# Columns of a modulation matrix loaded from ScalarE's queue instead of SyncE's, in a three-layer mixer kernel

## The chip, the cores and the metric

The kernel runs on one core of a Trainium2 chip. The metric is the device time of the whole program in microseconds, the median of several executions. The profiled execution is one more, taken by the hardware profiler; all times of rows below are its own, counted from its start.

## What is computed

A token stream x of 512 tokens by 2048 channels goes through three layers, all in 32-bit floats. Each layer takes a modulation from a condition vector, a product with a wide weight matrix, a mixer, a product back and a residual. In short:

```python
mod = silu(c) @ w_ada + b_ada                 # 2048 -> 3 x 2048: shift, scale, gate
h = norm(x) * (1 + scale) + shift
z = h @ w_in                                  # layer 1: 7184 columns
y = concat(spatial_gating(z...), forgetting_attention(z...)) @ w_out
x = x + gate * y
# layer 2: gated linear attention, both directions, with states from a context of
# 256 tokens (the context has a modulation of its own from a vector c_ctx), and a
# convolution of three taps; layer 3: means over windows of rows, four 512 x 512 products
x = layer_norm(alpha * x + gate * mixer(x * (1 + scale) + shift))
```

The modulation is a matrix-vector product: w_ada has 2048 rows and 6144 columns in each of the three layers, so it is as large as other weights, and each of its elements is used once (twice where the context needs the same columns).

## The kernel before, in words

All large products are written as a list of *groups* (GROUPS). A group is 512 output columns (or fewer) of one weight matrix, summed over 16 *tiles* of 128 rows. Each 32-bit weight tile is split into a high and a low part, and each product is three matmuls (high by high, high by low, low by high, L1010 to L1012 or L1019 to L1021). With four column blocks a tile is 12 matmuls; in the group f (112 columns) and in r (128 columns) it is 3, in ck (256 tokens) 6.

A tile goes through the engines so. SyncE loads pairs of tiles into w_raw, four pairs deep (`weights`, L292). ScalarE copies a tile to its high part in w_hi (L547, L571), four tiles ahead of TensorE. VectorE subtracts to make the low part in w_lo (L1399), after the high part. TensorE waits for the low part (`lo_done`) and for the operand's tile (`op_tile`). The high part of tile k is made when TensorE is done with tile k-4, so ScalarE's and VectorE's *step t* of a group works on tile t+4, for the last four steps on the next group's tiles.

The modulation's columns are computed beside these products. 28 groups have a *part*: 512 columns of w_ada, in 16 tiles. They are five runs of consecutive groups: va to the first v group (8 groups), gb to the third wo1 group (5), the first ck group alone (1), r to the first ev group (6), and the second egb group to the third xp group (8). In step t of such a group VectorE, after the low part, adds tile t of the part, scaled by the condition's entry, to an accumulator (`part_tile`, L1402, instructions L1415 for tile 0 and L1417 else; two per tile where the context's condition is added too). The columns come in pairs of tiles into a_raw, two pairs deep, so pair m may be loaded when tile 2m-3 has been accumulated, and it is wanted at tile 2m. After the group TensorE sums the accumulator over partitions, and VectorE takes the result (`take_part`).

Before the change SyncE issues these loads too (`modulation`, L303). Its `stream` issues the weight pairs of a group in order and puts the modulation pair m-3 behind weight pair m (LAG is 3), the last three pairs behind the next group's first weight pairs. SyncE waits on `part_tile` for the buffer before it issues. For `beside` (the groups of the gated attention's heads) a_raw holds other data, which SyncE writes to memory.

Where a group is the first to use an operand (va, wo1, r, wo2, xp), the operand's tiles are built while its steps run: ScalarE makes op_hi (L594), VectorE op_lo (L1498), and steps start at operand tile 4 (`early`). ScalarE also evicts most groups' results from PSUM at their end (L686 for va).

Of the kernel before, what the change touches and what calls it, by code (L numbers as in the profile page):

```python
# [5 lines left out]
P = 128  # L6
# [3 lines left out]
KT = D // P  # L10
GC = 512
# [6 lines left out]
GLA_HEADS, DK = 4, 256  # L18
# [3 lines left out]
RAW = 4  # L22
# [58 lines left out]
GROUPS, FIRST, CHUNKS = plan()  # L81
# [28 lines left out]
def early(n):  # L110


    if n and GROUPS[n - 1]["operand"] == GROUPS[n]["operand"] or GROUPS[n]["name"] == "cr":

        return 0
    return min(GROUPS[n]["kt"], KT - 4)
# [30 lines left out]
class Build:  # L147
# [42 lines left out]
    def at(self, word, *shape):  # L190
        n = 1
        for k in shape:
            n *= k
        assert word + n <= ARENA, (word, shape)
        v = self.arena[:, word:word + n]
        if len(shape) == 2:
            v = v.rearrange("p (a b) -> p a b", a=shape[0])
        if len(shape) == 3:
            v = v.rearrange("p (a b c) -> p a b c", a=shape[0], b=shape[1])
        return v  # L200

    def sem(self, name):
        if name not in self.sems:
            self.sems[name] = self.nc.alloc_semaphore(name)
        return self.sems[name]
# [9 lines left out]
def ordinal(n):  # L215

    return sum(x["part"] is not None for x in GROUPS[:n])
# [14 lines left out]
def sync_program(B, sp):  # L232
    A, sem, at = B.A, B.sem, B.at
# [35 lines left out]
    w_ada = A["w_ada"][0].rearrange("(k p) n -> p k n", p=P)  # L269
# [22 lines left out]
    def weights(n, m, r=0):  # L292

        g = GROUPS[n]
        slot = (g["kc"] // 2 + m) % RAW
        if g["kc"] + 2 * m >= 2 * RAW:

            sp.wait_ge(sem("lo_done"), r * 8 + (g["kc"] + 2 * m - 2 * RAW + 2))
        tiles = slice(2 * m, 2 * m + 2) if isinstance(r, int) else bass.ds(r * 8 + 2 * m, 2)
        sp.dma_start(B.w_raw[:, slot, :, 0:g["width"]],  # L300
                     B.weight(g)[:, tiles, g["col"]:g["col"] + g["width"]]).then_inc(B.w_in[slot], 16)

    def modulation(n, m):  # L303

        part, o = GROUPS[n]["part"], ordinal(n)
        if part is None:
            return
        src = A["w_ada"][0] if part < 12 else A["w_ada_2"][(part - 12) // 12]
        src = src.rearrange("(k p) n -> p k n", p=P)
        c = part % 12 * GC  # L310
        if o or m >= 2:

            sp.wait_ge(sem("part_tile"), KT * o + 2 * m - 2)
        sp.dma_start(B.a_raw[:, m % 2, :, :], src[:, 2 * m:2 * m + 2, c:c + GC]).then_inc(B.a_in[m % 2], 16)

    def stream(n, middle=None):


        pairs = GROUPS[n]["kt"] // 2
        before = n and GROUPS[n - 1]["part"] is not None  # L320
        if GROUPS[n]["part"] is None and not before and not middle and pairs == 8 and GROUPS[n]["name"] != "egb":
            with sp.Fori(0, 2) as r:
                for m in range(4):
                    weights(n, m, r)
            return
        for m in range(pairs):
            weights(n, m)
            if GROUPS[n]["name"] == "egb":
                conv_loads(GROUPS[n]["i"], m)
            if m < LAG and before and not (middle and m == 2):  # L330
                modulation(n - 1, 8 - LAG + m)
            if middle and m == 1:

                if before:
                    modulation(n - 1, 7)
                middle()
            if m >= LAG:
                modulation(n, m - LAG)

    def residual(n):  # L340

# [82 lines left out]
    def conv_loads(i, m):  # L424

        if i == 0 and m == 3:

            sp.wait_ge(sem("heads_done"), GLA_HEADS + 1)
            beside_store(1, GLA_HEADS - 1)
            sp.wait_ge(sem("beside_stored"), 16 * (2 * GLA_HEADS + 1))  # L430
        j = m - 3 if i == 0 else m + 5
        if 0 <= j < 8:
            if j >= CONV_SLOTS:

                sp.wait_ge(sem("conv_done"), j - CONV_SLOTS + 1)
            src = B.c_sp.rearrange("p (v h) (t s) -> p v (h t) s", v=4, t=4)
            sp.dma_start(at(AT_CONV, CONV_SLOTS, 4, S)[:, j % CONV_SLOTS, :, :], src[:, :, j, :])\
                .then_inc(B.sem(f"conv_in_{j}"), 16)
# [8 lines left out]
    for n, name in enumerate(names):  # L447
# [7 lines left out]
        if name in ("ua", "ga"):  # L455
            if g["i"] == 0:
                with sp.Fori(0, 2) as r:
                    attention_turn(r, name == "ga")
            continue
        stream(n, middles.get(n))  # L460
        if name == "xp" and g["i"] == 0:
            spill_stream(2)
# [36 lines left out]


N_ROW_LOADS = 12
LAG = 3


def start_step(n):
# [27 lines left out]
def scalar_program(B, act):  # L533
    nc, sem, at, ps, Y = B.nc, B.sem, B.at, B.ps, B.Y
# [4 lines left out]
    def high_tile(c, width):  # L539
        raw, fill = c // 2 % RAW, c // (2 * RAW)  # L540
        if c % 2 == 0:

            act.wait_ge(B.w_in[raw], 16 * (fill + 1))
        if c >= RING:

            act.wait_ge(sem("w_used"), c - RING + 1)
        Act(B.w_hi[:, c % RING, 0:width], B.w_raw[:, raw, c % 2, 0:width], ACT.Copy).then_inc(sem("hi_done"), 1)  # L547

    def step(n, t):

        c, k, width = GROUPS[n]["kc"], GROUPS[n]["kt"], GROUPS[n]["width"]
        after = GROUPS[n + 1]["width"] if n + 1 < len(GROUPS) else 0
        if t < k - 4:
            high_tile(c + 4 + t, width)
        elif after:
            high_tile(c + 4 + t, after)

    def ahead(n):

        c, k, width = GROUPS[n]["kc"], GROUPS[n]["kt"], GROUPS[n]["width"]  # L560
        after = GROUPS[n + 1]["width"] if n + 1 < len(GROUPS) else 0
        if k == KT and after == width and not early(n):
            with act.Fori(0, 2) as r:
                for t in range(c + 4, c + 12):
                    raw = t // 2 % RAW
                    if t % 2 == 0:

                        act.wait_ge(B.w_in[raw], r * 16 + 16 * (t // (2 * RAW) + 1))

                    act.wait_ge(sem("w_used"), r * 8 + (t - RING + 1))  # L570
                    Act(B.w_hi[:, t % RING, 0:width], B.w_raw[:, raw, t % 2, 0:width],  # L571
                        ACT.Copy).then_inc(sem("hi_done"), 1)
        else:
            for t in range(early(n), k):
                step(n, t)

    def conv_ahead(n):

        for t in range(KT):
            high_tile(GROUPS[n]["kc"] + 4 + t, GC)  # L580
            for j in range(8):
                if CONV_AT[j] == (GROUPS[n]["i"], t):
                    act.wait_ge(sem(f"conv_in_{j}"), 16)
                    x = at(AT_CONV, CONV_SLOTS, 4, S)[:, j % CONV_SLOTS, 3, :]
                    Act(x, x, ACT.Silu).then_inc(sem("conv_gate"), 1)

    def split_hi(operand, src, tok=S, tiles=KT, ready=None):

        if operand:

            last = max(x["kc"] + x["kt"] for x in GROUPS if x["operand"] == operand - 1)
            act.wait_ge(sem("w_used"), last)
        for t in range(tiles):
            Act(B.op_hi[:, t, 0:tok], src(t), ACT.Copy).then_inc(sem("op_high"), 1)  # L594
            if 4 <= t < 4 + early(first_use(operand)):
                step(first_use(operand), t - 4)
# [68 lines left out]
    for n, g in enumerate(GROUPS):  # L665
        name, i = g["name"], g["i"]
# [8 lines left out]
        if name == "egb":  # L675
            conv_ahead(n)
        else:
            ahead(n)
# [78 lines left out]
    for t in range(NT):  # L757
        for j in range(4):
            k = 4 * t + j
# [1276 lines left out]
def model_kernel(nc, A, out):  # L2036
    B = Build(nc, A, out)
    with nc.Block() as block:

        @block.sync  # L2040
        def _(sp):
            with nc.allow_non_contiguous_dma(reason="columns of small tables"):
                sync_program(B, sp)

        @block.gpsimd
        def _(pool):
            pool_program(B, pool)

        @block.scalar
        def _(act):  # L2050
            scalar_program(B, act)

        @block.vector
        def _(dve):
            vector_program(B, dve)

        @block.tensor
        def _(pe):
            tensor_program(B, pe)
# [38 lines left out]
```

## Time and profile before

| | |
|---|---|
| median of 3 runs | 3188.45 us (3185.68 to 3190.76) |
| the profiled execution's own time | 3190.58 us |
| its span in the profile | 3188.8 us |
| TensorE busy with matmuls | 2874.2 us, 90% |
| VectorE busy | 1772.7 us, 56% |
| ScalarE busy | 1054.5 us, 33% |
| moved by DMA | 451.17 MB, mean 141 GB/s |

The span is the profile's, the execution's own time is 1.8 us longer. Instructions that only issue a DMA or wait are not counted as busy. Groups start about every 44 us where a tile is 12 matmuls.

### The profile page before, as it was taken

Reading aid. Unit: us, or ns where it says so; the run is one execution under the profiler, and the core shown is the slowest. Engines: PE = TensorE matmul, PEld = TensorE weight load, DVE = VectorE, ACT = ScalarE, POOL = GpSimd, SP = SyncE. Lnnn points to the kernel's source line nnn. Section 1 sums busy time; section 2 is a strip of 40 time slices with the busy share of each in tenths; the row PEclk is TensorE's granted clock in tenths of the full one; section 3 lists DMA queues with packets and bytes.
Section 4 is the critical chain, followed back from the end, with each engine's and each line's share of the span. In section 5 each row is a group of like instructions: output and inputs, shape, how many; then the busy total and the mean of one; then the engine's idle time right before and its main releaser. Section 6 shows DMA issues by size and latency. Waiting matters only on the chain.

```text
span 3188.8 us, 36906 instructions
## 1 busy us (share of the span) xinstructions
PE 2874.2 (90%) x12667; PEld 2275.4 (71%) x12667; DVE 1772.7 (56%) x2777; ACT 1054.5 (33%) x1630; POOL 4.1 (0%) x10
## 2 busy tenths in 40 slices
PE   3499999989999988689999999999899699998995
PEld 2377887666777857468878686776788488887883
DVE  7857773444578536264427475473766576324443
ACT  2333222333323235332224434352332332223224
POOL 0000000000000000000000000000000000000000
PEclk8699999999999989789999999999999899999997
DMA  9766552212255526165532222223656274332331
GB/s 369 280 195 206 192 173 70 62 61 66 85 185 191 193 94 198 69 222 191 192 113 80 73 92 66 86 92 106 225 191 210 80 246 144 99 95 91 113 113 53
DMA packets 219351, 451.17 MB, mean 141 GB/s; under 512 B 23753, under 2 KB 29339, under 8 KB 214861
## 3 DMA queue, kind: packets, MB, share of 16 engines
q1 hardware_dynamic: 219212, 449.36, 42.6%
q8 instruction: 83, 1.36, 0.2%
q14 instruction: 56, 0.45, 0.0%
HBM read 422.01 MB, written 27.30 MB: 141 GB/s over the span
## 4 chain that ended last, share of the span: by engine, by line
PE 81%; DVE 6%; ACT 4%; issue 4%; DVEq 1%; DMA 1%; ACTq 1%; SPq 1%; PEldq 0%; PEld 0%
PE ps L1010 20%; PE ps L1012 19%; PE ps L1011 19%; PE ps L1019 4%; PE ps L1020 4%; PE ps L1021 4%; PE ps L1341 2%; PE ps L1063 2%; PE ps L1211 1%; PE ps L1219 1%; PE ps L989 1%; DVE acc L1584 1%; PE ps L1372 1%; PE ps L1375 1%; PE ps L1363 1%
## 5 line engine op out<-in xcount | busy, mean ns | idle before, releaser
L1010 PE MATMUL ps<-op_hi,w_hi 128*128 128x512 f32 (+2 forms) x2928 | 1177.1, 402 | 84.2 <-DVE op_lo L1498 43.7
L1012 PE MATMUL ps<-op_hi,w_lo 128*128 128x512 f32 (+2 forms) x2928 | 1154.5, 394 | 0.0
L1011 PE MATMUL ps<-op_lo,w_hi 128*128 128x512 f32 (+2 forms) x2928 | 1154.4, 394 | 0.0
L1399 DVE TENSOR_TENSOR w_lo<-w_raw,w_hi 128x512 fp32r<-128x512 f32 (+2 forms) x640 | 421.7, 661 | 620.9 <-ACT w_hi L571 414.3
L1010 PEld LDWEIGHTS ps<-op_hi,w_hi 128*128 128x128 f32 (+1 forms) x2928 | 560.7, 192 | 225.2 <-issue 54.4
L1012 PEld LDWEIGHTS ps<-op_hi,w_lo 128*128 128x128 f32 (+1 forms) x2928 | 559.6, 191 | 119.8
L1011 PEld LDWEIGHTS ps<-op_lo,w_hi 128*128 128x128 f32 (+1 forms) x2928 | 561.0, 192 | 112.7 <-issue 1.7
L571 ACT ACTIVATE w_hi<-w_raw 128x512 fp32r<-128x512 f32 x496 | 312.8, 632 | 969.4 <-PE ps L1012 802.6
L1417 DVE SCALAR_TENSOR_TENSOR acc<-a_raw,vec,acc 128x512 f32<-128x512 f32 x540 | 392.8, 746 | 19.6 <-DMA a_raw<-in_w_ada 19.5
L547 ACT ACTIVATE w_hi<-w_raw 128x512 fp32r<-128x512 f32 (+2 forms) x240 | 134.7, 565 | 357.6 <-PE ps L1012 276.2
L1019 PE MATMUL ps<-w_hi,op_hi 128*128 128x512 f32 x512 | 202.9, 396 | 27.4 <-DVE op_lo L1498 16.0
L1020 PE MATMUL ps<-w_hi,op_lo 128*128 128x512 f32 x512 | 201.3, 393 | 0.0
L1021 PE MATMUL ps<-w_lo,op_hi 128*128 128x512 f32 x512 | 201.0, 393 | 0.0
L1452 DVE TENSOR_TENSOR w_lo<-w_raw,w_hi 128x512 fp32r<-128x512 f32 x96 | 66.2, 693 | 161.0 <-ACT w_hi L571 160.7
L1019 PEld LDWEIGHTS ps<-w_hi,op_hi 128*128 128x128 f32 x512 | 97.3, 190 | 48.7 <-issue 16.2
L1879 DVE TENSOR_TENSOR w_lo<-w_raw,w_hi 128x512 fp32r<-128x512 f32 x128 | 83.3, 687 | 65.7 <-ACT w_hi L903 61.6
L1021 PEld LDWEIGHTS ps<-w_lo,op_hi 128*128 128x128 f32 x512 | 97.4, 190 | 20.7
L1020 PEld LDWEIGHTS ps<-w_hi,op_lo 128*128 128x128 f32 x512 | 97.4, 190 | 20.4 <-issue 0.2
L818 ACT ACTIVATE arena<-arena,small 128x128 f32<-128x128 f32 (+1 forms) x64 | 36.0, 563 | 195.0 <-DVE small L1811 195.0
L1584 DVE SCALAR_TENSOR_TENSOR acc<-arena,vec,acc 128x512 f32<-128x512 f32 x128 | 84.9, 743 | 22.6 <-ACT vec L658 11.5
L903 ACT ACTIVATE w_hi<-w_raw 128x512 fp32r<-128x512 f32 x128 | 75.7, 621 | 43.0 <-PE ps L1012 42.9
L938 ACT ACTIVATE arena<-arena 128x2048 f32<-128x2048 f32 x28 | 53.6, 1915 | 108.6 <-DVE arena L1925 108.6
(208 smaller groups left out, 2139.0 us busy)
## 6 DMA issues: line engine op xcount, KB each, us to landing
a_raw<-in_w_ada SPq DMA_DIRECT2D x224, 512.0 KB, 4.0
w_raw<-in_w_in_e SPq DMA_DIRECT2D x160, 512.0 KB, 4.6
w_raw<-in_w_in SPq DMA_DIRECT2D x112, 512.0 KB, 4.8
arena<-in_w_ada SPq DMA_DIRECT2D x64, 512.0 KB, 8.0
w_raw<-in_w_in_o SPq DMA_DIRECT2D x64, 512.0 KB, 3.7
w_raw<-in_w_out SPq DMA_DIRECT2D x32, 512.0 KB, 5.0
w_raw<-in_w_out_e SPq DMA_DIRECT2D x32, 512.0 KB, 4.9
w_raw<-in_w_out_o SPq DMA_DIRECT2D x32, 512.0 KB, 3.7
```

Of the source, the lines that this page charges most:

```text
L547: Act(B.w_hi[:, c % RING, 0:width], B.w_raw[:, raw, c % 2, 0:width], ACT.Copy).then_inc(sem("hi_done"), 1)
L571: Act(B.w_hi[:, t % RING, 0:width], B.w_raw[:, raw, t % 2, 0:width], ACT.Copy).then_inc(sem("hi_done"), 1)
L1010: mm(dst, hi[:, cols], B.op_hi[:, k, 0:tok], start=first, stop=False)
L1011: mm(dst, hi[:, cols], B.op_lo[:, k, 0:tok], start=False, stop=False)
L1012: last = mm(dst, lo[:, cols], B.op_hi[:, k, 0:tok], start=False, stop=last_t)
L1019: mm(dst, B.op_hi[:, k, rows], hi, start=first, stop=False)
L1020: mm(dst, B.op_lo[:, k, rows], hi, start=False, stop=False)
L1021: last = mm(dst, B.op_hi[:, k, rows], lo, start=False, stop=last_t)
L1399: V.tensor_tensor(B.w_lo[:, c % RING, 0:width], B.w_raw[:, c // 2 % RAW, c % 2, 0:width], B.w_hi[:, c % RING, 0:width].bitcast(f32), ALU.s ...
L1417: last = V.scalar_tensor_tensor(out=sums, in0=x, scalar=col, in1=sums, op0=ALU.mult, op1=ALU.add)
L1584: V.scalar_tensor_tensor(out=sums, in0=ring[:, s, v * GC:(v + 1) * GC], scalar=B.vec[:, bass.ds(r * 8 + (VEC["c"] + s), 1)], in1=sums, op0 ...
L1879: V.tensor_tensor(B.w_lo[:, c % RING, :], B.w_raw[:, c // 2 % RAW, c % 2, :], B.w_hi[:, c % RING, :].bitcast(mybir.dt.float32), ALU.subtract)\
```

## The change

The modulation loads are issued by ScalarE. In step t of a group with a part, behind the step's high part, it issues pair t/2 + 1 of that part for even t up to 12, and at t = 14 pair 0 of the next group's part if it has one. The first pair of a run's first group is issued at its step 0, just ahead of pair 1. ScalarE waits on `part_tile` as SyncE did. In the second egb group pairs 0 and 1 also wait until the last of a_raw's other data has been written to memory. SyncE issues weights alone; its groups with a part now run in a loop, ScalarE's groups with a part are written out.

```diff
@@ sync_program
-    def modulation(n, m):
-        ...
-        if o or m >= 2:
-            sp.wait_ge(sem("part_tile"), KT * o + 2 * m - 2)
-        sp.dma_start(B.a_raw[:, m % 2, :, :], src[:, 2 * m:2 * m + 2, c:c + GC]).then_inc(B.a_in[m % 2], 16)
 
     def stream(n, middle=None):
         pairs = GROUPS[n]["kt"] // 2
-        before = n and GROUPS[n - 1]["part"] is not None
-        if GROUPS[n]["part"] is None and not before and not middle and pairs == 8 and GROUPS[n]["name"] != "egb":
+        if not middle and pairs == 8 and GROUPS[n]["name"] not in ("egb", "wo2") and GROUPS[n]["kc"] >= 2 * RAW:
             with sp.Fori(0, 2) as r:
                 for m in range(4):
                     weights(n, m, r)
@@ 
             if GROUPS[n]["name"] == "egb":
                 conv_loads(GROUPS[n]["i"], m)
-            if m < LAG and before and not (middle and m == 2):
-                modulation(n - 1, 8 - LAG + m)
             if middle and m == 1:
-                if before:
-                    modulation(n - 1, 7)
                 middle()
-            if m >= LAG:
-                modulation(n, m - LAG)
@@ scalar_program
+    def modulation(n, m):
+        part, o = GROUPS[n]["part"], ordinal(n)
+        src = B.A["w_ada"][0] if part < 12 else B.A["w_ada_2"][(part - 12) // 12]
+        src = src.rearrange("(k p) n -> p k n", p=P)
+        c = part % 12 * GC
+        if GROUPS[n]["name"] == "egb" and m < 2:
+            act.wait_ge(sem("beside_stored"), 16 * (2 * GLA_HEADS + 1))
+        if o or m >= 2:
+            act.wait_ge(sem("part_tile"), KT * o + 2 * m - 2)
+        act.dma_start(B.a_raw[:, m % 2, :, :], src[:, 2 * m:2 * m + 2, c:c + GC]).then_inc(B.a_in[m % 2], 16)
+
+    def has_part(n):
+        return 0 <= n < len(GROUPS) and GROUPS[n]["part"] is not None
+
+    def modulation_step(n, t):
+        if t == 0 and has_part(n) and not has_part(n - 1):
+            modulation(n, 0)
+        if has_part(n) and t % 2 == 0 and t < 14:
+            modulation(n, t // 2 + 1)
+        if has_part(n) and t == 14 and has_part(n + 1):
+            modulation(n + 1, 0)
@@ step, ahead, conv_ahead
             high_tile(c + 4 + t, after)
+        modulation_step(n, t)
...
-        if k == KT and after == width and not early(n):
+        if k == KT and after == width and not early(n) and not has_part(n):
             with act.Fori(0, 2) as r:
```

## Rows read from the trace of the kernel before

**Rows 1.** The page, parts 1 and 4: busy time by engine, chain by engine.
```profile
PE 2874.2 (90%) x12667; PEld 2275.4 (71%) x12667; DVE 1772.7 (56%) x2777; ACT 1054.5 (33%) x1630; POOL 4.1 (0%) x10
...
PE 81%; DVE 6%; ACT 4%; issue 4%; DVEq 1%; DMA 1%; ACTq 1%; SPq 1%; PEldq 0%; PEld 0%
```

**Rows 2.** TensorE's waits: line, released by, us in total, times, longest.
```profile
PE ps L1010 <- DVE w_lo L1399: 13.7, 18, 3.1
```

**Rows 3.** Waits of SyncE's queue.
```profile
SPq L314 <- DVE acc L1417: 1052.2, 213, 54.4
```

**Rows 4.** The tile a_raw: instruction times in ns, idle time, DMA landing.
```profile
L314 SPq DMA_DIRECT2D a_raw<-in_w_ada x224: 367/368/1296, 115.7 to 2666.4; - x112
...
  DMA a_raw<-in_w_ada: 21.2, 20
...
DMA to landing us min/median/max: 3.7/4.0/12.3
```

**Rows 5.** Timeline of va: start, us, engine, line, instruction [idle before, released by].
```profile
138.20 0.61 ACT L547 ACTIVATE w_hi<-w_raw 128x512 fp32r<-128x512 f32 x1
...
139.54 0.48 DVE L1415 TENSOR_SCALAR acc<-a_raw,vec 128x512 f32<-128x512 f32 x1
...
142.84 0.63 ACT L547 ACTIVATE w_hi<-w_raw 128x512 fp32r<-128x512 f32 x1 [1.62 <-PE ps L1021]
...
145.52 0.69 DVE L1399 TENSOR_TENSOR w_lo<-w_raw,w_hi 128x512 fp32r<-128x512 f32 x1
...
150.94 0.63 ACT L547 ACTIVATE w_hi<-w_raw 128x512 fp32r<-128x512 f32 x1 [0.79 <-PE ps L1021]
```

**Rows 6.** Timeline of f and of the start of q.
```profile
223.91 0.37 SPq L314 DMA_DIRECT2D a_raw<-in_w_ada  x1
...
224.58 1.08 ACT L547 ACTIVATE w_hi<-w_raw 128x112 fp32r<-128x112 f32 x4
...
229.32 0.37 SPq L314 DMA_DIRECT2D a_raw<-in_w_ada  x1
...
233.22 0.75 DVE L1417 SCALAR_TENSOR_TENSOR acc<-a_raw,vec,acc 128x512 f32<-128x512 f32 x1 [0.91 <-DMA a_raw<-in_w_ada]
...
255.30 0.50 PE L1010 MATMUL ps<-op_hi,w_hi 128*128 128x512 f32 x1 [3.06 <-DVE w_lo L1399]
```

**Rows 7.** Timeline of the first ck group.
```profile
1204.61 2.17 ACT L571 ACTIVATE w_hi<-w_raw 128x512 fp32r<-128x512 f32 x4
...
1205.86 0.48 DVE L1415 TENSOR_SCALAR acc<-a_raw,vec 128x512 f32<-128x512 f32 x1
...
1211.78 0.75 DVE L1417 SCALAR_TENSOR_TENSOR acc<-a_raw,vec,acc 128x512 f32<-128x512 f32 x1 [1.04 <-DMA a_raw<-in_w_ada]
...
1228.03 0.75 DVE L1417 SCALAR_TENSOR_TENSOR acc<-a_raw,vec,acc 128x512 f32<-128x512 f32 x1 [0.21 <-DMA a_raw<-in_w_ada]
1228.70 0.69 DVE L1399 TENSOR_TENSOR w_lo<-w_raw,w_hi 128x512 fp32r<-128x512 f32 x1
```

**Rows 8.** Windows in ck: busy by engine, granted clock, DMA share, GB/s.
```profile
1215.00:1220.00 5.00, 5.00 (x24) 4.14 (x23) 4.21 (x7) 2.14 (x4) 0.00 (x0) 1.00 0.85 258
1220.00:1225.00 5.00, 5.00 (x24) 4.14 (x23) 3.64 (x6) 2.53 (x4) 0.00 (x0) 1.00 1.01 370
```

**Rows 9.** Timeline of r and of the start of ek.
```profile
1368.89 0.31 ACT L547 ACTIVATE w_hi<-w_raw 128x128 fp32r<-128x128 f32 x1 [4.64 <-DMA w_raw<-in_w_in_e]
...
1370.69 0.49 DVE L1415 TENSOR_SCALAR acc<-a_raw,vec 128x512 f32<-128x512 f32 x1 [1.18 <-DMA a_raw<-in_w_ada]
...
1392.13 0.47 PE L1010 MATMUL ps<-op_hi,w_hi 128*128 128x512 f32 x1 [0.35 <-issue]
```

**Rows 10.** Timeline of the second egb group and of the start of wo2.
```profile
2282.44 0.75 DVE L1417 SCALAR_TENSOR_TENSOR acc<-a_raw,vec,acc 128x512 f32<-128x512 f32 x1
...
2284.37 0.69 DVE L1399 TENSOR_TENSOR w_lo<-w_raw,w_hi 128x512 fp32r<-128x512 f32 x1
...
2312.39 0.76 PE L1010 MATMUL ps<-op_hi,w_hi 128*128 128x512 f32 x1 [9.30 <-DVE op_lo L1498]
```

More of the change, by code:

```diff
@@ L301, in weights @@
                      B.weight(g)[:, tiles, g["col"]:g["col"] + g["width"]]).then_inc(B.w_in[slot], 16)
-    def modulation(n, m):
[L305 to L310, printed above, removed]
-        if o or m >= 2:
-            sp.wait_ge(sem("part_tile"), KT * o + 2 * m - 2)
-        sp.dma_start(B.a_raw[:, m % 2, :, :], src[:, 2 * m:2 * m + 2, c:c + GC]).then_inc(B.a_in[m % 2], 16)
     def stream(n, middle=None):
         pairs = GROUPS[n]["kt"] // 2
-        before = n and GROUPS[n - 1]["part"] is not None
-        if GROUPS[n]["part"] is None and not before and not middle and pairs == 8 and GROUPS[n]["name"] != "egb":
+        if not middle and pairs == 8 and GROUPS[n]["name"] not in ("egb", "wo2") and GROUPS[n]["kc"] >= 2 * RAW:
             with sp.Fori(0, 2) as r:
@@ L501 @@
 N_ROW_LOADS = 12
-LAG = 3
 def start_step(n):
@@ L585, in conv_ahead @@
                     Act(x, x, ACT.Silu).then_inc(sem("conv_gate"), 1)
+            modulation_step(n, t)
     def split_hi(operand, src, tok=S, tiles=KT, ready=None):
```

## The prediction

> **What bounds the kernel now.** I read the page first. TensorE is busy for 90% of the span and makes 81% of the chain that ended last [rows 1]. So a change of load queues is worth only what it does where TensorE waits. The list of TensorE's waits comes next: the low parts of weight tiles (w_lo, VectorE, L1399) cost it 13.7 us in 18 waits on one line [rows 2]. They are few, and the timeline puts them where a modulation column is accumulated beside short tiles. The queue's own waits show the largest number, 1052.2 us in 213 waits of SyncE's L314 for VectorE's accumulation [rows 3]. The reader must not take it for a loss: a queue that waits costs nothing unless what stands behind it comes late. The tile view of a_raw has the size of the lateness: VectorE sat 21.2 us in 20 waits for these loads, a load takes 367 ns to issue and lands after 3.7 to 12.3 us, 4.0 in the median [rows 4].
>
> **Where there is cover.** VectorE makes low parts up to four tiles ahead of TensorE. In a group with 12 matmuls a tile a load that is late by three microseconds eats into that lead and nothing else. In groups with 3 or 6 matmuls a tile (f, ck, r) VectorE itself sets the pace, and lateness goes through.
>
> **What the change removes.** SyncE no longer waits for accumulation steps between weight loads. Weight slots become free at the low part of the same step, so each weight load goes out about one accumulation (0.7 us) plus one issue (0.4 us) earlier. Nothing in TensorE's 12-matmul groups waits for weights, so this is worth nothing there.
>
> **What it adds to ScalarE.** 224 issues of 0.37 us [rows 4] are 83 us. ScalarE is busy 33% [rows 1], mostly waiting for TensorE between tiles, so its idle time hides them. If an issue took the longest seen, 1.30 us [rows 4], an even step would still be 0.63 + 1.30 us, under the 2.7 us that 12 matmuls take (three tiles between 142.84 and 150.94 [rows 5]). ScalarE's new wait is for the accumulation of step t-1, which VectorE runs before the low part of step t. Behind it stand the high part of step t+1 and, at a group's end, the eviction. When VectorE catches up it needs about 1.26 us for a low part and an accumulation; ScalarE needs 0.37 + 0.63 us after the wait, so it stays ahead.
>
> **What it moves: the first loads of a run.** Before, a run's first two columns were loaded by SyncE while the former group still ran. Now they are issued at step 0 behind a high part, just before VectorE wants them. As price of one I take 3.9 us, from the issue at 229.32 to the accumulation that waited for it at 233.22 [rows 6]. There are five such starts.
> - va: high part at 138.20, accumulation at 139.54 [rows 5]. Issued 138.3 to 138.8, it lands at 142.2 to 142.7, so VectorE is 2.7 to 3.2 us late. The low part of tile 6 ends at 146.2, and TensorE asks for it at 150.94, when ScalarE's high part shows it done with tile 5 [rows 5]. The lead of 4.7 us covers this: 0, with 1.5 us to spare.
> - gb has 12 matmuls a tile and no operand to build, so more cover than va: 0.
> - ck (6 matmuls): high part 1204.61, accumulation 1205.86 [rows 7]. It lands at 1208.6 to 1209.1, +2.7 to +3.3 us. From there to the last low part at 1228.70 before took 22.84 us, of which 4.0 us were five waits for a_raw, the first 1.04 and the last 0.21 [rows 7]; 18.8 us is work. A load is issued two and a half tiles before its use, 3.15 us of work, so with a landing L each two loads cost L - 3.15 in waits; six loads cost 3(L - 3.15): 2.3 us at 3.9, 5.5 us at 5.0. The end is 1208.85 + 18.8 + 2.3 to 5.5 = 1229.9 to 1233.2, which is +1.2 to +4.5 less what VectorE had to spare (some 0.1 to 0.7). The DMA engines are full there (share 0.85 to 1.01) [rows 8], and two more loads fall into the stretch, but it also starts 2.9 us sooner. I take +2.1 (0.5 to 3.8).
> - r (3 matmuls, VectorE builds the operand): ScalarE's high part at 1368.89 itself waits 4.64 us for its weights. Issued at 1369.0 to 1369.2, the column lands at 1372.9 to 1373.1; before, 1370.69 [rows 9]. TensorE follows VectorE tile by tile until 1392.13 [rows 9]. I take +2.3 (2.0 to 3.5; the lower is the shortest landing of 3.7, the upper a landing of 5).
> - egb's second group: VectorE is late by an earlier evacuation, the load lands before it is wanted: 0.
>
> **The second load of each later group** is issued at step 0, behind the former group's eviction. Only f suffers: its column 1 went out at 223.91, now after the high part at 224.58, which stands behind the eviction of va's second group [rows 6]: +0.7 to +1.0. In f each pair of steps waits for its column (0.91 us at 233.22 [rows 6], one of eight), two buffers alternate, and the last pair uses the late one; VectorE's next work ends in TensorE's 3.06 us wait at 255.30 [rows 6]. So it goes through. A landing longer by 0.5 us would add 0.25 x 7 pairs; one of 3.7 us takes 0.7 away. I take +1.2 (0 to 2.8).
>
> **ScalarE held back.** In the second egb group VectorE has no idle time and its end sets TensorE's restart at 2312.39 after 9.30 us [rows 10]. ScalarE now waits for the accumulation that ends at 2283.2 (started 2282.44), issues, and has the high part ready at 2284.2; VectorE wants it at 2284.37 [rows 10]. It just fits; there are two such places. +0.2 (0 to 1.2, with 1.0 us issues).
>
> **Sum:** 0 + 0 + 2.1 + 2.3 + 1.2 + 0.2 = +5.8 us. The profiled execution took 3190.58 us (span 3188.8 and 1.8 around it), so its like after the change would be 3196.4; it stood 2.1 us over the median. Against the median of 3188.45 the forecast is 3194.2 us.
>
> **Two queues.** The landing of a_raw is the number in dispute. In the before trace the column goes out first and the weights 0.41 us behind it on one queue (229.32 and its like), now the weights go first by about a microsecond on another. The trace has no such pair, so the landing is bounded by the shortest of 3.7 us below, and above by 5 us, an estimate between the median of 4.0 and the longest of 12.3 [rows 4]. The Trainium skill (DMA: Bandwidth & Descriptors, Queues, rings and completion order) says that each DMA engine goes round-robin between queues by packets; by it the column would share the engines with the weights ahead of it, and the sum would lean to the contention case. The same page (Issuing engines are not separate DMA queues) says that issuing from several engines saves only issue time; by it alone the steady state would not change, and no run here shows either yet.
>
> **The rivals.**
> - Contention (18%): columns land after 5 us beside weights. Then ck +3.8, r +3.5, f +1.0 + 7 x 0.55 = +4.8, egb +1: +13, 3201.5 us. For it: a DMA share of 1.01 in ck [rows 8]. Against: the bytes are the same. It decides from a landing of 4.6 us on.
> - Cover holds (22%): the issue overlaps the high part, loads land in 3.7 us, ck's end is caught up; r alone and something of f stay: +2, 3190.5 us.
> - Faster (10%): a column no longer queues among weights. If it landed at once, f would lose its eight waits of about 0.9 us, -7.3 us, 3181 us with the starts hidden. It decides only if the landing falls from 3.9 to under 2.5 us, and the shortest of 224 was 3.7 [rows 4].
> - My forecast has 50%, with a range of its own of 3190.5 to 3198.
>
> **The numbers.** No change that can be told is within 0.2%, 3182.1 to 3194.8. The forecast lies at its upper edge: 27 of its 50 fall inside, 23 above. Same 0.27 + 0.22 = 0.49; slower 0.23 + 0.18 = 0.41; faster 0.10. The range 3186 to 3203 leaves out most of the faster case and the tail of contention.
>
> **What would show it.** Right: VectorE's first accumulation in ck near 1209 and in r near 1373, counted from the same high parts, each with a wait for a_raw of some 3 us; no new TensorE stall in va, gb, wo1, wo2, xp; TensorE's restart after f one microsecond later. Wrong: a TensorE stall inside a 12-matmul group, ScalarE's high parts held for more than 1 us where VectorE then waits, issues on ScalarE far over 0.5 us, or a landing that leaves 3.7 to 4.6 us.

## The result, and the profile after

The changed kernel took 3202.74 us (median of 5 runs, 3200.66 to 3204.54) against 3188.45 us: a ratio of 1.0044, with a 95% interval of 1.0029 to 1.0059. It is slower by 14.3 us (9 to 19). The forecast was 3194.2 us with a range of 3186 to 3203, so the time lies 0.3 us inside the range's upper end. Slower had a chance of 0.41, the same time had 0.49. The profiled execution has a span of 3201.2 us, 12.4 us more than before.

I read the page first: busy time by engine, then the chain by engine.

```profile
PE 2879.8 (90%) x12667; PEld 2278.4 (71%) x12667; DVE 1772.8 (55%) x2777; ACT 1053.5 (33%) x1630; POOL 4.1 (0%) x10
...
PE 79%; DVE 6%; ACT 4%; issue 4%; DMA 3%; DVEq 1%; ACTq 1%; SPq 1%; PEldq 0%; PEld 0%
```

The work is the same as before [rows 1]; DMA went from 1% to 3% of the chain. The tile view of a_raw says which DMA. Its columns are those of [rows 4], and below them stands who waited.

```profile
L539 ACTq DMA_DIRECT2D a_raw<-in_w_ada x224: 374/374/483, 137.0 to 2678.6; - x112
...
  DMA a_raw<-in_w_ada: 41.5, 29
...
  ACT w_hi L525: 44.6, 16
...
  ACT op_hi L600: 15.4, 5
...
DMA to landing us min/median/max: 3.7/4.6/16.5
```

An issue takes 374 ns on ScalarE, 7 ns more than on SyncE. A load lands after 4.6 us in the median instead of 4.0, and after 16.5 us at worst. VectorE waited 41.5 us for these loads instead of 21.2. TensorE's waits for low parts:

```profile
PE ps L1016 <- DVE w_lo L1405: 20.8, 18, 3.9
```

That is 7.1 us more than [rows 2], in as many waits. To place the loss I took pairs of events that both timelines have and subtracted the lengths between them. The names used below are: *f*, from TensorE's first matmul of va at 132.06 us (times of the kernel before) to its first of q at 255.30; *ck*, from 1206.00 to the context's first product at 1293.28; *context*, from there to 1341.18; *r*, from 1362.21 to 1662.09; *xp*, from 2539.89, TensorE's first matmul of xp, to 2897.60. They are 1.41, 1.03, 1.70, 2.20 and 5.74 us longer. Outside these names two stretches of the changed kernel's profile differ by more than 0.5 us, both along with another granted clock of TensorE: from 1662.09 to 2539.89 it is 1.83 us shorter, from 2897.60 to 2948.84 it is 0.74 us longer (last section). The largest is one that the prediction priced at nothing. Here is the first xp group in the changed kernel's timeline:

```profile
2563.14 0.39 ACTq L539 DMA_DIRECT2D a_raw<-in_w_ada  x1
2563.21 0.34 SPq L290 DMA_DIRECT2D x_spill<-Y  x1
...
2579.67 0.75 DVE L1423 SCALAR_TENSOR_TENSOR acc<-a_raw,vec,acc 128x512 f32<-128x512 f32 x1 [10.25 <-DMA a_raw<-in_w_ada]
...
2583.19 0.63 ACT L600 ACTIVATE op_hi<-arena 128x512 fp32r<-128x512 f32 x1 [9.66 <-DVE acc L1423]
```

SyncE issues a 4 MB store of x (`spill_stream(2)`, the line behind the first xp group's `stream`) 0.07 us after ScalarE issued a column pair. The pair lands 16.5 us later, when the store is through. VectorE, which builds the operand in the same steps, stands for 10.25 us, and so does ScalarE behind its wait for the accumulation. TensorE waits 3.90 us for a low part, which is the longest of the row above. That is not yet 5.74 us; the rest is in TensorE's clock. Behind the wait it drops to the lower of its two levels. These are 3.4 us of the changed kernel, and the same 3.4 us of the kernel before, 5.70 us earlier (columns as in [rows 8]):

```profile
2583.00:2586.40 3.40, 3.40 (x10) 2.63 (x9) 3.40 (x7) 2.19 (x4) 0.00 (x0) 0.51 0.86 284
```

```profile
2577.30:2580.70 3.40, 3.40 (x17) 2.81 (x16) 1.65 (x3) 0.63 (x1) 0.00 (x0) 1.00 1.05 397
```

TensorE gets through 10 matmuls instead of 17. Half speed for 3.4 us costs 1.7 us, and 3.90 + 1.7 is 5.6. All six profiles in which TensorE stands still for 3.8 to 4.3 us here have this drop behind it (changed, e2, e7, e9, e10, e12), none of the other eight has it.

This is the same place in the kernel before:

```profile
2557.42 0.37 SPq L314 DMA_DIRECT2D a_raw<-in_w_ada  x1
...
2562.07 0.37 SPq L314 DMA_DIRECT2D a_raw<-in_w_ada  x1
...
2562.48 0.47 SPq L290 DMA_DIRECT2D x_spill<-Y  x1
...
2579.05 0.75 DVE L1417 SCALAR_TENSOR_TENSOR acc<-a_raw,vec,acc 128x512 f32<-128x512 f32 x1 [4.99 <-DMA a_raw<-in_w_ada]
```

The changed kernel is 5.72 us late when it comes to this place. The column at 2557.42 goes out at 2563.14 there, exactly as much later (TensorE's first matmul of xp, at 2539.89, is 5.73 us later): ScalarE is not late with it. The store at 2562.48 would fall on 2568.20 and stands at 2563.21, 5.0 us early. Before, SyncE's wait for accumulation step 5, ahead of column pair 4, had held the store back; the change took the wait away with the load.

How the two transfers share the engines stands in the DMA view of a window, here 2569 to 2571 us, in the middle of the store (queue 1 is SyncE's, queue 10 ScalarE's; the columns are packets, MB, and the time they took as a share of 16 engines' time):

```profile
q1 hardware_dynamic: 30, 0.98, 114.9%
q10 hardware_dynamic: 30, 0.06, 8.4%
```

The queues get the same number of packets, 30 and 30; in the windows of 2 us beside it they are 19 and 19, 19 and 20, 29 and 28. A packet of the store is 0.98 MB / 30 = 33 KB, a whole row of x (16 tiles of 2 KB). A packet of the column is 2 KB. So the column gets a sixteenth of the bytes. The store has 128 such packets and the column 256: taking turns one for one, the column is not through before the store is. The Trainium skill (DMA: Bandwidth & Descriptors, Queues, rings and completion order) has the rule, round-robin between queues by packets, and the trace agrees packet by packet; by that rule the price hangs on the length of a row.

### The profile page after: what moved, and what is told of

It reads as the page before. It is cut to its first block, busy times and chain, and to the rows that moved or that the text cites. A ratio compares the mean times of both kernels' runs of the same rounds, so it can differ in the third digit from the quotient of the medians.

```text
span 3201.2 us, 37322 instructions
## 1 busy us (share of the span) xinstructions
PE 2879.8 (90%) x12667; PEld 2278.4 (71%) x12667; DVE 1772.8 (55%) x2777; ACT 1053.5 (33%) x1630; POOL 4.1 (0%) x10
## 4 chain that ended last, share of the span: by engine, by line
PE 79%; DVE 6%; ACT 4%; issue 4%; DMA 3%; DVEq 1%; ACTq 1%; SPq 1%; PEldq 0%; PEld 0%
PE ps L1016 19%; PE ps L1018 19%; PE ps L1017 19%; PE ps L1025 3%; PE ps L1027 3%; PE ps L1026 3%; DMA a_raw<-in_w_ada 2%; PE ps L1347 2%; PE ps L1069 2%; PE ps L1217 1%; PE ps L1225 1%; PE ps L995 1%; PE ps L1378 1%; PE ps L1381 1%; DVE acc L1590 1%
## 5 line engine op out<-in xcount | busy, mean ns | idle before, releaser
L525 ACT ACTIVATE w_hi<-w_raw 128x512 fp32r<-128x512 f32 (+2 forms) x560 | 335.3, 603 | 1001.3 <-PE ps L1018 813.5
L576 ACT ACTIVATE w_hi<-w_raw 128x512 fp32r<-128x512 f32 x176 | 111.2, 632 | 317.9 <-PE ps L1018 228.2
L909 ACT ACTIVATE w_hi<-w_raw 128x512 fp32r<-128x512 f32 x128 | 75.7, 622 | 44.3 <-PE ps L1018 44.3
```

## The experiments

The theories: A, SyncE's removed waits let the store (and the weights) go ahead of the columns. B, ScalarE's own waits and issues in front of its high parts cost the time. C, two queues in themselves make a landing longer. P, a column's share beside a store follows from the length of the packets; Q, a store blocks a load whatever its packets.

Each ratio is to the kernel before in the same set, with its 95% interval. The changed kernel has 1.0044 and, run again (last but two), 1.0043, some 14 us; an interval is about 3 us wide on either side. So the stretches of the profiles decide between theories, and the ratios the sums. The table has the five named stretches, in us longer than in the kernel before's profile. They hold steps of the clock too: the stretches between them move by up to 4.8 us from profile to profile (255.30 to 1206.00 in e5, shorter), in kernels of both kinds, so a difference of less than 2 us in one profile is not a finding by itself.

| run | ratio | f | ck | context | r | xp |
|---|---|---|---|---|---|---|
| changed | 1.0044 | 1.41 | 1.03 | 1.70 | 2.20 | 5.74 |
| e10, changed again | 1.0043 | 2.93 | 0.90 | 1.70 | 2.25 | 5.73 |
| e1, store waits | 1.0017 | 1.88 | 1.26 | 1.70 | 2.30 | 1.17 |
| e2, starts early | 1.0027 | 2.75 | 0.91 | 1.70 | -1.29 | 5.81 |
| e3, SyncE's waits kept | 1.0029 | 3.20 | 2.73 | 0.01 | 3.10 | 1.13 |
| e4, before, store first | 1.0006 | 0.66 | -0.12 | 1.70 | -0.02 | 0.63 |
| e5, store in rows of 2 KB | 1.0019 | 3.61 | 1.27 | 3.40 | 2.29 | -0.09 |
| e12, store in 8 pieces | 1.0033 | 2.34 | 1.48 | 1.70 | 2.36 | 5.83 |
| e6, starts and later store | 1.0004 | 3.67 | 1.47 | 1.70 | -1.47 | 0.79 |
| e7, f and ck by SyncE | 1.0023 | 1.04 | 1.24 | 1.69 | 1.93 | 6.19 |
| e9, two issues a pair | 1.0039 | 2.61 | 1.40 | 1.70 | 2.10 | 5.82 |
| e11, three mends | 1.0001 | 0.16 | 1.18 | 1.70 | -1.45 | -0.21 |
| e8, before, r early | 0.9984 | 0.63 | -0.23 | 3.40 | -1.59 | -0.04 |

**e1: the store waits again.**

```diff
         if name == "xp" and g["i"] == 0:
+            sp.wait_ge(sem("part_tile"), KT * ordinal(n) + 6)
             spill_stream(2)
```

> The changed kernel with one wait more: SyncE issues the 4 MB store of x in the first xp group only when VectorE has accumulated tile 5 of that group's part, where it stood before the change. Theory A (the store overtook the columns, because SyncE no longer waited for accumulations): VectorE's wait of 10.25 us for a_raw and TensorE's of 3.90 us in the operand's build go, 5 to 6 us less than the changed kernel, about 3197 us; a shorter wait of some 5 us may come back at tile 8 or 10. Theory B (ScalarE, with its waits and issues in front of its own high parts, is what costs the time there): nothing changes, 3202 to 3203 us.

Ratio 1.0017 (1.0008 to 1.0026), 3196.59 us: some 8 us less than the changed kernel, of which xp has 4.6. Theory A holds. The timeline shows what is left of it:

```profile
2567.07 0.34 SPq L290 DMA_DIRECT2D x_spill<-Y  x1
2567.07 0.42 ACTq L540 DMA_DIRECT2D a_raw<-in_w_ada  x1
...
2581.48 0.75 DVE L1424 SCALAR_TENSOR_TENSOR acc<-a_raw,vec,acc 128x512 f32<-128x512 f32 x1 [7.88 <-DMA a_raw<-in_w_ada]
```

The next pair is caught in its place, for 14.4 us, but it is wanted two steps later, when most of the operand is built, and TensorE loses 1.2 us instead of 5.7.

**e4: in the kernel before, the store ahead of a column.**

```diff
             weights(n, m)
+            if GROUPS[n]["name"] == "xp" and GROUPS[n]["i"] == 0 and m == 7:
+                spill_stream(2)
...
-        if name == "xp" and g["i"] == 0:
-            spill_stream(2)
```

> The kernel before, with one thing changed: in the first xp group SyncE issues the store of x right behind weight pair 7, ahead of column pair 4 instead of behind it. If the store's place alone is what costs, column pair 4 lands only with the store, 12 us or more after its issue, VectorE waits some 5 to 6 us at tile 8 of the operand's build and the kernel is 1 to 5 us slower than before, 3190 to 3194 us. If it takes the second queue, nothing is lost: 3188.5 us.

Ratio 1.0006 (0.9997 to 1.0015): xp is 0.63 us longer. Column pair 4, issued at 2562.02 behind the store on the same queue, is used at 2575.88 after a wait of 7.31 us. So one queue delays a column as a second one does (13.8 us); what costs little here is that pair 3 was already out at 2557.37. The loss needs both, the early store and a column that is not clearly ahead of it: here pair 3 was 0.93 us ahead on the store's own queue and landed after 4.4 us, in the changed kernel it was 0.07 us ahead on another queue and landed after 16.5 us.

**e3: SyncE keeps its waits, without the loads.**

```diff
+    def modulation(n, m):
+        part, o = GROUPS[n]["part"], ordinal(n)
+        if part is not None and (o or m >= 2):
+            sp.wait_ge(sem("part_tile"), KT * o + 2 * m - 2)
```

> The changed kernel, but SyncE keeps all its waits for accumulation steps where they stood before the change, without the loads. Theory A (weights and the store go out too early, ahead of the columns): the store's 5.7 us go, and what f (1.4 us) and ck (1.0 us) lost goes too, since a weight pair again follows a column instead of leading it: 8 us less, about 3194.5 us, the rest being the late start of r. Theory C (two queues in themselves make a landing longer): the median landing of a_raw stays 4.6 us, only the store's part goes, 3197 us. Theory B (ScalarE's holding): 3202 us or more, since a wait is added.

Ratio 1.0029 (1.0018 to 1.0040). xp came back, as A and C had it. But f and ck did not, they became longer (3.20 and 2.73), and the median landing rose to 5.1 us. With its waits SyncE issues the weights in the same moment in which ScalarE issues the column. Two loads of 512 KB then share the engines, and the column is the one that lands last: taking away the weights' lead brings neither f nor ck back. The traces show what that does to a column and the weight pair issued next to it, in medians:

| | column lands after | weights land after | both are there, from the first issue |
|---|---|---|---|
| before: one queue, column 0.4 us ahead (200 pairs) | 4.0 us | 4.9 us | 5.3 us |
| changed: two queues, weights 0.3 to 0.7 us ahead (52 pairs) | 4.7 us | 3.9 us | 5.2 us |
| e3: two queues, within 0.15 us of each other (107 pairs) | 5.3 us | 4.7 us | 5.3 us |

So theory C holds in part only. The column lands later, but the two loads together take as long on two queues as on one. What the second queue changes is who comes home first: on one queue the column did, because SyncE issued it first; now the weights do, and over the whole program their median landing fell from 4.7 to 3.7 us while the column's rose from 4.0 to 4.6. No stretch is shorter for it. Whether a column issued 0.4 us ahead on ScalarE's queue would land after 4.0 us again was not run.

**e2: the runs at ck and r start a group early.**

```diff
+        if GROUPS[n]["name"] == "cr" or GROUPS[n]["name"] == "cv" and GROUPS[n]["i"] == 1:
+            if t in (10, 12):
+                modulation(n + 1, t // 2 - 5)
+            return
```

> The changed kernel, with pairs 0 and 1 of the runs that start at ck and r issued by ScalarE at steps 10 and 12 of the group before. If late starts cost what the prediction says, r's first accumulation waits no longer than before the change (3.38 us to 1.2 or none) and TensorE starts ek 2.0 to 3.5 us sooner; in ck the trace of the changed kernel shows no wait at the first accumulation, so nothing there. Together 2 to 3.5 us less than the changed kernel, 3199 to 3201 us. The rival, that r is held by its weights, which stand behind the stores of x and of the states: the high part at 1374 waits as long and only 0 to 1 us is won.

Ratio 1.0027 (1.0017 to 1.0037), 5 us less than the changed kernel. r is 3.5 us shorter, ck as long as it was. In the changed kernel r's start looks like this:

```profile
1373.98 0.31 ACT L525 ACTIVATE w_hi<-w_raw 128x128 fp32r<-128x128 f32 x1 [4.38 <-DMA w_raw<-in_w_in_e]
1373.98 0.90 ACTq L539 DMA_DIRECT2D a_raw<-in_w_ada  x2
...
1377.99 0.49 DVE L1421 TENSOR_SCALAR acc<-a_raw,vec 128x512 f32<-128x512 f32 x1 [3.38 <-DMA a_raw<-in_w_ada]
```

and with the pair issued early, beside a high part that still waits 4.38 us for its weights:

```profile
1373.24 0.48 DVE L1426 TENSOR_SCALAR acc<-a_raw,vec 128x512 f32<-128x512 f32 x1
```

VectorE no longer waits. The kernel before had lost 1.3 us there as well: its column stood behind r's weights and these behind the stores of x and of the states.

**e5: the store in rows of 2 KB.**

```diff
+        if m == 2:
+            for t in range(KT):
+                sp.dma_start(B.x_sp[:, t, :], B.Y[:, t, :]).then_inc(sem("spilled"), 16)
+            return
```

> The changed kernel; the store of x in the first xp group stands where the change put it, but goes out as 16 stores of one tile each, so that a row of it is 2 KB, as long as a row of a column pair, and not 32 KB. Theory P (two queues share the DMA engines packet by packet, so a column of short packets gets a small share beside a store of long ones: 522 packets with 1.02 MB against 679 with 5.23 MB in the window of the store): the column issued with the store lands after 5 to 8 us instead of 16.5, VectorE waits 0 to 2 us instead of 10.25, TensorE not at all, 5 us less than the changed kernel. Theory Q (a store blocks a load whatever its packets): the wait of 10 us stays, and the time with it.

Ratio 1.0019 (1.0010 to 1.0028); xp is as short as before (-0.09).

```profile
2561.88 0.39 ACTq L543 DMA_DIRECT2D a_raw<-in_w_ada  x1
...
2569.32 0.75 DVE L1427 SCALAR_TENSOR_TENSOR acc<-a_raw,vec,acc 128x512 f32<-128x512 f32 x1 [1.16 <-DMA a_raw<-in_w_ada]
```

The column lands after 7.4 us, in a window in which the engines are nearly as full (DMA share 0.88 from its issue to its landing, 0.96 in the changed kernel's like window). Theory P has its number. This run changed the length of a row and the size of a piece together, so the next one changes the piece alone.

**e12: the store in 8 pieces of 16 partitions, rows as long as they were.**

```diff
+            for d in range(8):
+                rows = slice(16 * d, 16 * d + 16)
+                sp.dma_start(B.x_sp[rows, :, :], B.Y[rows, :, :]).then_inc(sem("spilled"), 16)
```

> The changed kernel; the store of x in the first xp group goes out as 8 stores of 16 partitions each (512 KB, the size of a column pair), whose rows stay 32 KB long. The run with rows of 2 KB changed two things at once, the length of the rows and the size of a piece; this one changes the piece alone. If the length of the rows decides how the engines are shared (theory P), the column issued with the store lands after 12 to 17 us as in the changed kernel and the xp stretch stays 4 to 6 us longer than before. If it is the piece, it lands after 5 to 9 us and the stretch is within 1 us of before.

Ratio 1.0033 (1.0020 to 1.0046). Neither answer came clean. The column lands after 8.0 us (issued at 2560.38, used at 2568.34), against my 12 to 17. Yet xp stays 5.83 us longer. The window from 2566 to 2568 us shows why the column got through:

```profile
q1 hardware_dynamic: 31, 0.49, 147.3%
q10 hardware_dynamic: 208, 0.39, 50.9%
```

ScalarE's queue gets 208 packets here, and the store's has 15 of 32 KB (the 0.49 MB; the other 16 of its 31 are under 512 bytes). So the turns one for one hold only while both queues have packets waiting. A piece has 16 rows, as many as there are engines, and between pieces ScalarE's queue has them to itself. The row of 32 KB still goes in one packet, but few others stand behind it. By these two runs the column's price is the length of a row times the rows that are queued; that is a reading, no run varied the number of queued rows alone. The store became the slow one: its issues stretch over 21.4 us and its last piece lands 29.9 us after the first issue, instead of 15.9 us, the second group's weights stand behind it, ScalarE waits 10.82 us for them before it can make a high part, and TensorE stands still for 3.99 us, with the clock's drop behind it:

```profile
2591.68 0.63 ACT L530 ACTIVATE w_hi<-w_raw 128x512 fp32r<-128x512 f32 x1 [10.82 <-DMA w_raw<-in_w_in_o]
...
2593.13 0.47 PE L1021 MATMUL ps<-op_hi,w_hi 128*128 128x512 f32 x1 [3.99 <-issue]
```

So this stretch is as long as the changed kernel's for another reason.

**e7: the columns beside f and ck issued by SyncE.** `modulation`, with its waits, is back in SyncE's `stream` at its old places and returns at once for other groups; ScalarE's returns for these.

```diff
+        if GROUPS[n]["name"] not in ("f", "ck") or GROUPS[n]["part"] is None:
+            return
```

> The changed kernel, but the columns beside the two short-tile groups f and ck are issued by SyncE with its waits, as before the change; all others stay with ScalarE. If two queues that share the engines are what makes a landing longer beside 512 KB weights, f and ck give back what they lost, 1.4 and 1.0 us in the profile: 2.4 us less than the changed kernel, and no landing over 4.3 us in these groups. If the loss there came of ScalarE's held-back high parts, the same. If it was the scatter of one profile, f and ck stay where they are.

Ratio 1.0023 (1.0014 to 1.0033). f is 1.04 us longer than before, and ck 1.24. Over all profiles, f has 0 to 1.04 where SyncE issues (before, e4, e7, e8, e11; mean 0.50) and 1.41 to 3.67 where ScalarE does (nine profiles, mean 2.71). They do not overlap: f costs 2.2 us. VectorE's own waits for a_raw in f say the same without the clock in them: 5.5 to 6.2 us in the five profiles with SyncE, 7.7 to 9.5 us in the nine with ScalarE, 7.67 against 5.48 in the changed kernel. For ck the answer is open: 0.90 to 1.48 with ScalarE (nine profiles without e3, mean 1.21), -0.23 to 0 in three profiles with SyncE, but 1.24 in this one, where VectorE waits 2.01 us for one column. VectorE's waits for a_raw in ck add up to 2.9 to 5.0 us in the four profiles with SyncE and to 5.2 to 5.8 us in the nine with ScalarE. I had expected no landing over 4.3 us in these groups; in ck they go up to 6.5 us on SyncE's queue too. The time is some 7 us less than the changed kernel's by the ratios, of which the profile's f and ck show 0.2 us; the rest is not explained.

**e9: two issues for each pair.**

```diff
+        for h in range(2):
+            act.dma_start(B.a_raw[:, m % 2, h, :], src[:, 2 * m + h, c:c + GC]).then_inc(B.a_in[m % 2], 16)
```

> The changed kernel, with each column pair loaded by two issues of one tile instead of one of two tiles: 448 issues on ScalarE instead of 224, some 83 us more of its queue's time, the same bytes. If the issues are hidden in ScalarE's idle time, as the prediction has it, the time stays within 3 us of the changed kernel. If ScalarE's queue is a cost in itself (0.4 us a pair in front of high parts that are wanted), the operand builds and the short-tile groups lengthen by 0.4 us a pair, 20 to 30 pairs, 8 to 12 us in all.

Ratio 1.0039 (1.0025 to 1.0052), the changed kernel's within its interval. An issue took 453 ns in the median, so ScalarE spent over 100 us more. Against the changed kernel's two profiles the only stretch that is clearly longer is ck, by 0.4 us, and the 8 to 12 us that a costly issue would have added are not there. ScalarE's time is free here, to some 3 us.

**e10: the changed kernel again.**

> The changed kernel once more, with nothing changed, beside the others of this set: a ratio to the kernel before of 1.003 to 1.005. In the second profile the stretches show what is scatter: xp +5.7 us and r +2.2 us against the kernel before should come again, f between +1.4 and +3.7 us, ck between +0.9 and +2.7 us; the context stretch between 1293 and 1341 us is scatter if it moves by a microsecond or more.

Ratio 1.0043 (1.0029 to 1.0056). xp, r and the context stretch repeat to 0.05 us, f does not (1.41 and 2.93). Of f's difference 0.57 us lies in the first 8 us of va, with which the stretch begins (granted clock 0.79 and 0.73), and 1.05 us in VectorE's waits for a_raw in f (7.67 and 8.72 us).

**e6, e11: the mends together.** e6 is e2 with the store behind weight pair 2 of the second xp group. e11 is e2 and e5, with f's columns issued by SyncE.

```diff
+        if GROUPS[n]["name"] == "xp" and GROUPS[n]["i"] == 1:
+            for m in range(8):
+                weights(n, m)
+                if m == 2:
+                    spill_stream(2)
+            return
```

> The changed kernel with both mends: ck's and r's first two column pairs are issued one group early by ScalarE, and the store of x goes behind weight pair 2 of the second xp group, some 10 us later. The first has won 3.5 us against the changed kernel in the stretch from r's first matmul to 1662 us, the second should win 5.7 us in xp: 9 us together, a ratio to the kernel before of 1.001 to 1.002. If the store merely collides with the next column there, VectorE waits some 8 us at tile 12, which 12-matmul tiles cover.

> The changed kernel with three mends: ck's and r's first pairs issued one group early, the store of x in the first xp group in 16 stores with rows of 2 KB, and the columns beside f issued by SyncE as before. Against the changed kernel r wins 3.7 us, xp 5.8, f 2.2: 11.7 us. If that is all that the change costs, the time is that of the kernel before less r's 1.5 us and plus ck's 1 us, a ratio of 1.000 (0.999 to 1.001). If something unseen remains, it stays at 1.0015 or more.

e6: 1.0004 (0.9994 to 1.0013). e11: 1.0001 (0.9992 to 1.0011), 3191.06 us. In e6 the store catches a pair for 14.7 us and VectorE waits 8.00 us, and the tiles of 12 matmuls cover it but for 0.8 us. The ratio is a little better than the 1.001 to 1.002 that I expected. e11's stretches give back what the three causes had taken, and the time is that of the kernel before. Nothing unseen of more than 3 us is left.

**e8: the kernel before, r's first two pairs ahead of r's weights.**

```diff
         stream(n, middles.get(n))
+        if n + 1 == FIRST["r"]:
+            modulation(n + 1, 0)
+            modulation(n + 1, 1)
```

> The kernel before, with r's first two column pairs issued by SyncE ahead of r's own weights, and so ahead of the stores of x and of the states, instead of behind weight pairs 3 and 4. The same edit in the changed kernel made the stretch from r's first matmul to 1662 us 3.5 us shorter than the changed kernel, 1.3 us shorter than the kernel before. The stretch should be 1.3 us shorter here too: 3187.2 us, a ratio of 0.9996. If the columns are not what r waits for, nothing changes.

Ratio 0.9984 (0.9974 to 0.9995), 3187.06 us against 3191.61 in its set: faster than both kernels. r is 1.59 us shorter, which is 0.0005 of the 0.0016 and lies at the interval's edge; no stretch of the profile shows the rest.

## Why the prediction's range held and its size did not

The range held, but by luck: the time lies 0.3 us inside it, and the largest part of the loss is in a group where the prediction had none. By its own signs the mechanism was wrong: a new TensorE stall in xp and a stall inside a 12-matmul group were among them, and VectorE's first accumulation in ck did not wait. The terms of r, gb and egb were right, va's result too; the size, 14 us and not 6, was not. By its own steps:

- **"Nothing in TensorE's 12-matmul groups waits for weights, so this is worth nothing there"**, and with it xp at 0: this step failed, and it is the largest term, 5.7 us. I asked what the earlier weight loads would bring and not what else stands behind the removed waits in SyncE's queue. The 4 MB store did. Both timelines, e1, e5 and e11 show it. The row that should have warned me was there before: the load that took 12.3 us to land [rows 4] was the next column issued behind this store, at 2566.72. Of the 5.7 us, 3.9 are TensorE's wait and 1.7 the clock behind it; no step of the prediction had the clock.
- **f, +1.2 (0 to 2.8):** inside its bounds at 2.2 us, by another way. Column 1 did not go out later. It was issued at 223.54, 0.67 us before the high part at 224.21, while ScalarE's eviction still ran; before, it was issued at 223.91, 0.67 us before the high part at 224.58, and the wait was the same (1.08 us at 227.32, before 1.07). What cost was the landing: from tile 8 on, when SyncE streams full weight tiles, pairs land after 5.4 and 5.6 us, and VectorE waits 2.49 us at 237.34. That is the contention rival's mechanism, in one half of the group.
- **The price that the faster rival had, 7.3 us for f's eight waits:** misread. Before, f has six such waits, 5.5 us together.
- **ck, +2.1:** 1.2 us, by another way. The step "issued at step 0 behind a high part" failed. The start was not late: ScalarE's queue issued both pairs at 1203.86 and 1204.28, 3.1 and 2.7 us before the high part that the program has ahead of them, and the first accumulation did not wait. Whether the 1.2 us come from the lost first place on the queue or are scatter is open (e7).
- **r, +2.3:** 2.2 us, as worked out: the pair went out with the high part at 1373.98 and landed 4.0 us later. e2 took it away.
- **va, gb at 0 and egb's second group at +0.2:** right in what they cost (egb's wait before wo2 is 9.64 us instead of 9.30). In va VectorE waits 0.88 us and not 2.7 to 3.2, since the pair was issued at 137.05, 1.6 us ahead of the high part; TensorE does not wait.
- **The issues hidden:** right (e9).
- **The price of a landing:** I took 3.9 us, with the contention case from 4.6 us on. It is 4.6 us in the median. The rival's total of 3201.5 us was close by chance: it had ck +3.8, r +3.5, f +4.8 and egb +1, and nothing in xp.
- Three more steps of the span's difference go with the granted clock (last section): +1.70 us in the context stretch, -1.83 us between 1662.09 and 2539.89, +0.74 us between 2897.60 and 2948.84. They add up to 0.6 us.

The terms 2.2 + 1.2 + 2.2 + 5.7 make 11.3 us, inside the interval of 9 to 19.

## What to carry to other kernels

Before you take a wait out of a queue, list all that stands behind it there, the large stores first: the wait may be what keeps them out of another load's way. Price a load beside a store by packets, not by bytes: rows of 32 KB starve another queue's rows of 2 KB, and cutting the store into short rows mended it (e5). On the store's own queue a load behind it waits as well (13.8 us in e4). A load that is wanted soon belongs ahead of its competitors on one queue; here the two loads together took 5.3 us on one queue and on two, and the second queue only gave away who came first. And when a stall is priced, look at the granted clock behind it: here 3.9 us of waiting cost 5.6.

## What the runs showed of the hardware

- While both have packets waiting, two queues get the DMA engines packet for packet (30 and 30, 19 and 19, 29 and 28), whatever a packet holds: 33 KB against 2 KB here. With the store in pieces it was 208 against 31. A 512 KB load issued at the same time as the 4 MB store landed after 14.4 us (e1) to 17.0 us (e7).
- Two loads of 512 KB issued within 0.7 us of each other are both there after 5.2 to 5.3 us, from one queue or from two; the medians are in e3's table.
- ScalarE's sequencer issues a DMA before the ACTIVATEs that stand ahead of it have run: in ck the two issues come 3.1 and 2.7 us before the high part that the program has first. In r, where that high part had to wait for its weights, the issue came with it.

```profile
1203.86 0.37 ACTq L539 DMA_DIRECT2D a_raw<-in_w_ada  x1
1203.92 0.70 ACT L654 ACTIVATE Y<-Y,vec 128x512 f32<-128x512 f32 x1
...
1206.98 1.65 ACT L525 ACTIVATE w_hi<-w_raw 128x512 fp32r<-128x512 f32 x3
```

- The context stretch is 0.0, 1.7 or 3.4 us longer than in the first profile, and nothing between, in kernels of both kinds. The granted clock goes with it. Windows of 10 us from the context's first product on, of the kernel before and of e8 (columns as in [rows 8]):

```profile
1293.30:1303.30 10.00, 9.94 (x16) 3.60 (x16) 0.00 (x0) 0.02 (x1) 0.00 (x0) 0.70 0.01 3
```

```profile
1293.50:1303.50 10.00, 10.00 (x13) 4.07 (x14) 0.00 (x0) 0.00 (x0) 0.00 (x0) 0.55 0.01 3
```

TensorE gets 0.70 of its full clock in the one and 0.55 in the other, a mixture of its two levels (1.0 is 2.4 GHz, 0.5 is 1.2), and TensorE had the full clock in the 10 us ahead of it, busy for 8.6 of them, in both. Most kernels here have the step of 1.7 us, with columns from either queue, so it is not booked on the change. The same holds for the -1.83 us from 1662.09 on: its first 8 us are 1.59 us shorter in the changed kernel, with a granted clock of 1.00 instead of 0.79, and e8, which loads from SyncE alone, has it too. Of the +0.74 us from 2897.60 on that is not shown: the granted clock of its first 7.6 us is 0.70 instead of 0.78, and the six profiles with 0.65 to 0.70 there all have their columns from ScalarE.
